# Two 64-row heads in one group of matmuls, by turns, in a two-block transformer kernel

## Chip, core and metric

One Trainium2 chip, one of its cores. The metric is the device time of one execution of the whole kernel, in microseconds (us). All tensors are float32. The kernel runs 256 tokens of width 1024 through two stacked blocks, and reads some 357 MB of weights from memory while it does so.

## What is computed

The first block has two layers. Each has a mixer (retention with 4 heads of 128, and stick-breaking attention with 8 heads of 64) and a gated feed-forward. The second block has two layers of feed-forward, mixer, cross attention to 256 memory rows, and feed-forward. The mixer of its first layer holds forgetting attention (8 heads of 64) and differential attention (4 heads, each of two halves of 64); that of its second layer a short convolution and a banded attention (8 heads of 64). The parts that the change touches, cut to what matters:

```python
# stick-breaking, per 128-query block, 8 heads of d = 64
z = einsum('bqhd,bkhd->bhqk', qb, kk) * d ** -0.5
log_one_minus = where(mask, log_sigmoid(-z), 0)
suffix = cumsum(log_one_minus, reverse) - log_one_minus
A = where(mask, exp(log_sigmoid(z) + suffix), 0)
out = einsum('bhqk,bkhd->bqhd', A, vv)
# differential, 4 heads, j = 0, 1 the two halves of 64
s = einsum('bqhjd,bkhjd->bhjqk', q, k) * 64 ** -0.5
p = softmax(where(allowed, s, -inf))
out = einsum('bhqk,bkhe->bqhe', p[:, :, 0] - lam * p[:, :, 1], v)
```

## The kernel before

**The frame.** Almost all of the work is matmuls of 256 tokens with streamed weights. A weight unit (128 x 1024 numbers) comes by DMA into one of 4 buffers RAW; ScalarE (ACT) rounds it to a high part WH (line 1049), VectorE (DVE) makes the low part WL = RAW - WH (line 1270), and there are 5 pairs WH/WL. TensorE (PE) then multiplies high by high, high by low and low by high, 512 columns each (lines 780 to 782), and adds them up in the PSUM tiles M. A "step" of the plan is three such matmuls for both halves of the tokens, so six instructions.

**The small work.** Attention, transposes and norms are small steps that are laid between those big matmuls. Their results go to four other PSUM banks, AUX. The class `Plan` gives each small step a place in time, `at`, counted in the steps just described, sorts all of them by it, and each engine then works through its own list strictly in that order. ACT and DVE have lists of their own, sorted by `at` plus a delay for the kind of step (`LATER`). Before its matmuls a small step on PE waits until the bank that it got is free (semaphore `aux_out`); when the matmuls are through it raises `aux_full`. The bank is the one whose last user is thought to be done first: each user is taken to hold it until `at` plus `HELD` (3.0 for both kinds of scores below).

**Stick-breaking (`first_mixer`, twice).** A projection leaves two heads on the 128 partitions, the first on rows 0 to 63, the second on rows 64 to 127. For the pair hp (0 to 3) and its head hh (0, 1) there are these steps, with b = e0 + 3.5 * (2 hp + hh):
- `st_z` at b: the scores, three float32 matmuls of 64 rows and 128 columns (lines 874 to 876; each shows as two matmul instructions);
- ACT and DVE turn them into logarithms (lines 1151 to 1157, 1429 to 1434); `st_p` at b + 3.0 splits the result (ACT line 1162, DVE line 1437);
- `st_s` at b + 4.9: the suffix sums on PE (lines 885 to 888), then DVE line 1442, ACT line 1166 and, as `st_a`, DVE line 1446;
- `st_o`, once for the pair, at 11.2 past the first head's b: probabilities by values (lines 900 to 902), the first head into partitions 0 to 63 of the bank, the second into 64 to 127; all three matmuls of the first head come before those of the second. ACT line 1169 and DVE line 1306 empty the bank.

**Differential attention (`even_mixer`, once).** Head h (0 to 3) starts at b = e0 + 5.0 h. Its halves are on rows 0 to 63 and 64 to 127. `df_s` at b and at b + 1.5 are the scores, two float32 matmuls each (line 929 with 128 columns, line 930 with 256). Mask, row maximum (DVE lines 1485 to 1498) and exponential (ACT lines 1200, 1201) follow; `df_p` at b + 4.6 combines both halves (DVE lines 1507 to 1519); `pt` at b + 6.2 turns the result on PE (line 962), `df_o` at b + 7.4 multiplies by the values (lines 973 to 975).

**Forgetting and banded attention (`heads`).** `hg_o` (lines 988, 989) multiplies probabilities by values for two heads as `st_o` does, into the two halves of the partitions of one bank.

Of the kernel before, what the change touches and what calls it, by code (L numbers as in the profile page):

```python
# [14 lines left out]
P = 128  # L15
# [127 lines left out]
class Step:  # L143
    def __init__(self, kind, at, rank):
        self.kind, self.at, self.rank = kind, at, rank
        self.place = self.n = self.bank = self.use = self.hi_n = self.m_n = self.p_n = 0
        self.first_use = False


# [7 lines left out]
class Tmp:  # L157
    def __init__(self, first):
# [6 lines left out]
LATER = {  # L165
    "conv": (0.0, 0.9), "turn": (0.5, 1.0), "tq": (0.5, 0.0), "gains": (0.5, 1.0), "rope": (0.0, 0.6), "ff": (0.0, 0.5),
    "hq": (0.0, 1.3), "ret_s": (0.0, 0.7), "ret_o": (0.9, 1.5), "rg": (0.0, 0.6), "st_z": (0.7, 1.9), "st_p": (0.0, 0.5),
    "st_s": (1.1, 0.6), "st_o": (0.8, 1.2), "df_s": (2.0, 0.8), "hg_s": (2.2, 1.1), "cx_s": (2.2, 1.4), "pt": (0.5, 0.0),
    "cx_pt": (0.6, 0.0), "df_o": (0.8, 0.0), "hg_o": (0.8, 1.2), "cx_o": (1.1, 1.7), "cu1": (0.0, 0.4), "cu_l": (0.0, 0.8),
    "cu2": (0.8, 0.0), "cv": (1.8, 0.0), "su_sin": (0.5, 0.0),  # L170
}
HELD = {"turn": 1.6, "tq": 1.0, "ret_s": 1.2, "ret_o": 1.2, "st_z": 3.0, "st_s": 1.5, "df_s": 3.0, "hg_s": 3.5,
        "cx_s": 2.5}


class Plan:
# [31 lines left out]

    def order(self, ntmp):
        steps = sorted(self.steps, key=lambda s: (s.at, s.rank, s.seq))  # L210
        act, dve = (sorted(steps, key=lambda s: (s.at + LATER.get(s.kind, (0.0, 0.0))[i], s.rank, s.seq)) for i in range(2))
        for i, s in enumerate(steps):
            s.place = i
        counts, use, busy = {}, [0] * 4, [-1e9] * 4
        for i, s in enumerate([s for s in act if s.kind in HALVED]):
            s.hi_n = i + 1
        for i, s in enumerate([s for s in dve if s.kind in ("df_s", "hg_s", "cx_s")]):
            s.m_n = i + 1
        for i, s in enumerate([s for s in dve if s.kind in ("df_p", "hg_p", "cx_p")]):
            s.p_n = i + 1  # L220
        for s in steps:
            counts[s.kind] = s.n = counts.get(s.kind, 0) + 1
            if s.kind in BANKED:
                b = min(range(4), key=lambda b: busy[b])
                use[b] += 1
                s.bank, s.use = b, use[b]
                busy[b] = s.at + HELD.get(s.kind, 1.5)
        ends = [-1] * ntmp
        for b in sorted(self.tmps, key=lambda b: b.first.place):
            b.i = next(i for i in range(ntmp) if ends[i] < b.first.place)  # L230
            ends[b.i] = b.final.place
        for s in steps:
            if s.kind == "mm":
                assert s.src.place < s.place, (s.c.name, s.kt)
        found = [s for s in dve if s.kind in ("ret_v", "hq", "bo_v")]
        assert [s.var for s in act if s.kind == "rsq"] == found
        self.for_pe, self.for_act, self.for_dve = steps, act, dve
# [162 lines left out]
    def first_mixer(self, l, S):  # L400
# [4 lines left out]
        for which, dst in (("rq", QT), ("rk", KT)):  # L405
            c = self.chunk(f"{which}{l}", B, 0, KD, lab)
            s = self.evict_x("rope", c, nm)
# [7 lines left out]
        e0 = c.end + 2.0  # L415
        for h in range(4):
            z = self.add("ret_s", e0 + 2.5 * h)
# [9 lines left out]
        v = self.add("ret_v", e0 + 12.0)  # L427
# [7 lines left out]
        for which, dst, f in (("sq", SQ, 0.125), ("sk", SK, 1.0)):  # L435
            c = self.chunk(f"{which}{l}", B, 0, KD, lab)
            s = self.evict_x("plainx", c, nm)
# [4 lines left out]
        e0 = c.end + 1.0  # L442
        prev = self.spl_prev
        for hp in range(4):
            zs = []
            for hh in range(2):
                i = 2 * hp + hh
                b = e0 + 3.5 * i
                z = self.add("st_z", b)
                z.q, z.k = (x[64 * hh:64 * hh + 64, hp, :] for x in (SQ, SK))  # L450
                z.turned = [self.turned[f"{w}{l}{t}"] for w in ("sq", "sk") for t in range(T)]
                z.sv = sv
                z.x = self.tmp(z)
                z.sp = self.DS[:, i % 2, 0:384]
                g = self.add("st_p", b + 3.0)
                g.z, g.prev = z, prev
                g.sh, g.sl = S["SPL"][:, 0:384], S["SPL"][:, 384:768]
                q = self.add("st_s", b + 4.9)
                q.z, q.p = z, g
                prev = q  # L460
                q.a = self.add("st_a", b + 6.7)
                q.a.s = q
                zs.append(q)
            o = self.add("st_o", b + 7.7)
            o.ss = zs
            for q in zs:
                q.z.x.final = o
            o.v = [SV[:, :, hp * P + hh * 64:hp * P + hh * 64 + 64] for hh in range(2)]
            o.hi, o.lo = A[0][:, 8 + hp, :], A[1][:, 8 + hp, :]
            self.made[f"sb{l}_", hp] = o  # L470
# [4 lines left out]
        for gi, which in enumerate(("gr", "gs")):  # L475
            for n in range(2):
                c = self.chunk(f"{which}{l}", B, 0, KD, lab)
                s = self.evict("gate", c, nm)
# [4 lines left out]
        for n in range(2):  # L483
            c = self.chunk(f"rg{l}", B, 0, KD, lab)
            s = self.evict("rg", c, nm)
# [6 lines left out]
            for j in range(2):  # L492
                k = 4 * n + 2 * j
                blocks = [RET[:, t, (k + q) * P:(k + q + 1) * P] for q in range(2) for t in range(T)]
                self.turn(c.end + 1.5 + 0.5 * j, "rg", s, blocks, A, k, None, f"ra{l}_", k)
        for n in range(2):
# [8 lines left out]
            for j in range(2):  # L505
                s = self.turn(c.end + 2.5 + 0.5 * j, "mer2", m2, None, B, 4 * n + 2 * j, 0.5, f"mg{l}_", 4 * n + 2 * j)
# [31 lines left out]
    def even_mixer(self, S, lab, lab_o):  # L538
# [3 lines left out]
        z = self.add("zero", self.now, 0)  # L542
# [19 lines left out]
        e0 = c.end + 3.5  # L562
        for h in range(4):
            b = e0 + 5.0 * h
            ss = []
            for j in range(2):
                s = self.add("df_s", b + 1.5 * j)
                s.q, s.k = (x[64 * j:64 * j + 64, h, :] for x in (QB, KB))
                s.turned = [self.turned[x] for x in ("bq0", "bq1", "bk0", "bk1")]
                s.vals = bv  # L570
                s.m, s.sm, s.rc = self.small(2), self.small(2), self.small(2)
                s.e = self.tmp(s)
                ss.append(s)
            f = self.add("df_p", b + 4.6)
            f.ss, f.nl = ss, self.small(2)
            t = self.add("pt", b + 6.2)
            ss[1].e.final = t
            t.source, t.maker, t.e = "df_p", f, ss[0].e
            ss[0].e.final = t
            t.x = self.tmp(t)  # L580
            o = self.add("df_o", b + 7.4)
            o.pt = t
            t.x.final = o
            o.v = VB[:, :, h * P:(h + 1) * P]
            o.dst = [BO[:, t_, h * P:(h + 1) * P] for t_ in range(T)]
            o.bs = [BS[:, 4 * t_ + h:4 * t_ + h + 1] for t_ in range(T)]
        v = self.add("bo_v", e0 + 24.5)
# [167 lines left out]
def tensor(e, k):  # L755
    p = k.p
# [3 lines left out]
    for s in p.for_pe:  # L760
        b = s.bank
        if s.kind in BANKED:
            aux = p.AUX[b]
        if s.kind == "mm":
# [12 lines left out]
            out = p.M[c.banks[s.t]][:, 0:s.ncol]  # L777
# [4 lines left out]
            i = e.matmul(out, s.lo, wh, start=False, stop=s.final)  # L782
# [84 lines left out]
        elif s.kind == "st_z":  # L867
# [3 lines left out]
                    e.wait_ge(k.aux_out[x.bank], x.use)  # L871
            if s.use > 1:
                e.wait_ge(k.aux_out[b], s.use - 1)
            e.matmul(aux[:, 0:128], s.k[:, 0:128], s.q[:, 0:128], start=True, stop=True)  # L874
            e.matmul(aux[:, 128:256], s.k[:, 128:256], s.q[:, 128:256], start=True, stop=True)
            e.matmul(aux[:, 256:384], s.k[:, 0:128], s.q[:, 128:256], start=True, stop=True).then_inc(k.aux_full[b], 1)
        elif s.kind == "st_s":
            if s.n == 1:
                e.wait_ge(k.unr_made, 1)
# [9 lines left out]
        elif s.kind == "st_o":  # L889
# [4 lines left out]
            e.wait_ge(k.st_prob, s.ss[1].a.n)  # L894
            if s.use > 1:
                e.wait_ge(k.aux_out[b], s.use - 1)
            for hh in range(2):
                x, v = p.TMP[s.ss[hh].z.x.i], s.v[hh]
                out = aux[64 * hh:64 * hh + 64, :]
                e.matmul(out[:, 0:128], v[:, 0, :], x[:, 0:128], start=True, stop=True)  # L900
                e.matmul(out[:, 128:256], v[:, 0, :], x[:, 256:384], start=True, stop=False)
                i = e.matmul(out[:, 128:256], v[:, 1, :], x[:, 128:256], start=False, stop=True)
            i.then_inc(k.aux_full[b], 1)
        elif s.kind == "cu1":
# [17 lines left out]
        elif s.kind == "df_s":  # L922
# [3 lines left out]
                    e.wait_ge(k.aux_out[x.bank], x.use)  # L926
            if s.use > 1:
                e.wait_ge(k.aux_out[b], s.use - 1)
            e.matmul(aux[:, 0:128], s.q[:, 0:P], s.k[:, 0:128], start=True, stop=True)
            e.matmul(aux[:, 128:384], s.q[:, P:256], s.k[:, 0:256], start=True, stop=True).then_inc(k.aux_full[b], 1)  # L930
        elif s.kind == "hg_s":
            for x in s.turned:
                if x not in seen:
# [42 lines left out]
        elif s.kind == "hg_o":  # L976
# [3 lines left out]
                e.wait_ge(k.m_out[vals.c.banks[1]], vals.c.use[1])  # L980
            if s.use > 1:
                e.wait_ge(k.aux_out[b], s.use - 1)
            for hh in range(2):
                pt, v = s.pts[hh], s.v[hh]
                e.wait_ge(k.aux_out[pt.bank], pt.use)
                x = p.TMP[pt.x.i]
                out = aux[64 * hh:64 * hh + 64, :]
                e.matmul(out[:, 0:256], v[:, 0, :], x[:, 0:256], start=True, stop=False)
                i = e.matmul(out[:, 128:256], v[:, 1, :], x[:, 256:384], start=False, stop=True)
            i.then_inc(k.aux_full[b], 1)  # L990
        elif s.kind == "cx_s":
# [897 lines left out]
```

## Time and profile before

| | |
|---|---|
| time, median of 3 runs | 2081.2 us (2080.53 to 2081.85) |
| the profiled execution's own time | 2080.47 us |
| its span, first to last instruction | 2078.3 us |
| PE matmuls busy | 2056.5 us (99%), 9627 instructions |
| PE weight loads busy | 1683.9 us (81%) |
| DVE busy | 1234.5 us (59%) |
| ACT busy | 1113.1 us (54%) |
| granted TensorE clock | 1.000 |
| DMA, mean | 173 GB/s |

The profile is of one execution. The start times of the matmuls can be relied on; their ends are modelled, and successive matmuls overlap. So a matmul's cost is best read as the distance from its start to the next one's start. A row of the timeline that merges several instructions of one line has their number at its end (x2), and its first number is the start of the first.

### The profile page before, as it was taken

The numbers are of one execution on the slowest core, as the hardware profiler recorded it, in microseconds if no ns is written. First come the engines' busy times: TensorE is split into PE (matmuls) and PEld (weight loads), VectorE is DVE, ScalarE is ACT, GpSimd is POOL, SyncE is SP. The second block draws the span as 40 slices with busy tenths as digits, with TensorE's granted clock in tenths as the row PEclk, the third lists the DMA queues.
The fourth block names the chain that finished last, engine by engine and source line by source line (L and its number), as shares of the span: only waits on it lengthen the run. The fifth ranks groups of instructions, "written<-read, shape, count | busy, mean of one in ns | idle before, by whom it ended". The sixth has DMA issues, their size and how long they took to land.

```text
span 2078.3 us, 25155 instructions
## 1 busy us (share of the span) xinstructions
PE 2056.5 (99%) x9627; PEld 1683.9 (81%) x9627; DVE 1234.5 (59%) x1721; ACT 1113.1 (54%) x1682; POOL 36.3 (2%) x60
## 2 busy tenths in 40 slices
PE   8999999999999999999999999999999999999999
PEld 6877888888778888888887888888888888788887
DVE  6576665565657555655557765655555466655553
ACT  5565544445665544654456665544444465665442
POOL 0000100000000000000000000000000000000000
PEclk9999999999999999999999999999999999999999
DMA  7545566555545665566564344665666563545553
GB/s 249 156 139 167 177 186 185 186 170 170 148 157 179 203 189 191 183 189 187 187 164 141 123 156 145 185 183 188 185 185 187 188 192 127 176 136 163 184 188 131
DMA packets 258215, 359.76 MB, mean 173 GB/s; under 512 B 16909, under 2 KB 152289, under 8 KB 258097
## 3 DMA queue, kind: packets, MB, share of 16 engines
q1 hardware_dynamic: 256016, 352.75, 54.5%
q0 software_dynamic: 2080, 5.41, 0.8%
q8 instruction: 77, 1.26, 0.2%
q14 instruction: 42, 0.34, 0.0%
HBM read 357.04 MB, written 1.06 MB: 172 GB/s over the span
## 4 chain that ended last, share of the span: by engine, by line
PE 95%; DVE 2%; ACT 1%; issue 1%; POOL 0%; DMA 0%; SPq 0%; DVEq 0%; ACTq 0%
PE M L780 29%; PE M L782 28%; PE M L781 28%; PE AUX L822 3%; PE AUX L836 1%; DVE WL L1270 1%; PE AUX L1022 1%; PE AUX L1000 1%; PE AUX L947 1%; ACT WH L1049 1%; PE AUX L962 0%; PE AUX L874 0%; DMA RAW<-in_w_in 0%; PE AUX L953 0%; DVE RET L1453 0%
## 5 line engine op out<-in xcount | busy, mean ns | idle before, releaser
L1270 DVE TENSOR_TENSOR WL<-RAW,WH 128x1024 fp32r<-128x1024 f32 x669 | 815.9, 1222 | 660.7 <-ACT WH L1049 657.9
L1049 ACT ACTIVATE WH<-RAW 128x1024 fp32r<-128x1024 f32 x669 | 706.3, 1058 | 670.5 <-PE M L782 664.1
L780 PE MATMUL M<-WH,Bh 128*128 128x512 f32 x1792 | 719.9, 402 | 3.9 <-DVE WL L1270 3.9
L782 PE MATMUL M<-WH,Bl 128*128 128x512 f32 x1792 | 700.4, 391 | 0.0
L781 PE MATMUL M<-WL,Bh 128*128 128x512 f32 x1792 | 699.5, 390 | 0.0
L780 PEld LDWEIGHTS M<-WH,Bh 128*128 128x128 f32 x1792 | 337.2, 188 | 73.5 <-DVE WL L1270 4.9
L782 PEld LDWEIGHTS M<-WH,Bl 128*128 128x128 f32 x1792 | 336.7, 188 | 72.6
L781 PEld LDWEIGHTS M<-WL,Bh 128*128 128x128 f32 x1792 | 337.7, 188 | 63.4
L1078 ACT ACTIVATE AS<-M,KEEP 128x256 f32<-128x256 f32 x132 | 55.3, 470 | 101.0 <-PE M L782 97.6
L780 PE MATMUL M<-WH,MTh 128*128 128x512 f32 x128 | 55.1, 430 | 0.0
L782 PE MATMUL M<-WH,MTl 128*128 128x512 f32 x128 | 50.5, 395 | 0.0
L781 PE MATMUL M<-WL,MTh 128*128 128x512 f32 x128 | 50.5, 394 | 0.0
L1328 DVE SCALAR_TENSOR_TENSOR X<-M,X 128x512 f32<-128x512 f32 x48 | 30.9, 686 | 20.8 <-PE M L782 20.7
L1099 ACT ACTIVATE Bh<-AUX,GTt 128x256 fp32r<-128x256 f32 x48 | 22.8, 474 | 29.0 <-PE AUX L822 29.0
L1295 DVE SCALAR_TENSOR_TENSOR Bl<-AUX,GTt,Bh 128x256 fp32r<-128x256 f32 x48 | 23.2, 483 | 25.3 <-ACT Bh L1100 25.3
L822 PEld LDWEIGHTS AUX<-CC,X 128*128 128x128 f32 x192 | 22.9, 144 | 15.2 <-issue 9.2
L780 PE MATMUL M<-WH,FA0h 128*128 128x512 f32 x88 | 34.5, 392 | 0.0
L780 PE MATMUL M<-WH,GA0h 128*128 128x512 f32 x88 | 34.5, 392 | 0.0
L780 PE MATMUL M<-WH,LA0h 128*128 128x512 f32 x88 | 34.5, 392 | 0.0
L780 PE MATMUL M<-WH,GA1h 128*128 128x512 f32 x88 | 34.5, 392 | 0.0
L780 PE MATMUL M<-WH,LA1h 128*128 128x512 f32 x88 | 34.3, 390 | 0.0
L780 PE MATMUL M<-WH,FA1h 128*128 128x512 f32 x88 | 34.3, 390 | 0.0
(405 smaller groups left out, 2515.4 us busy)
## 6 DMA issues: line engine op xcount, KB each, us to landing
RAW<-in_ffn_w_in SPq DMA_DIRECT2D x352, 256.0 KB, 3.2
RAW<-in_w_in SPq DMA_DIRECT2D x104, 512.0 KB, 3.8
RAW<-in_w_gate_up SPq DMA_DIRECT2D x176, 256.0 KB, 3.3
RAW<-in_ffn_w_out SPq DMA_DIRECT2D x88, 512.0 KB, 3.6
RAW<-in_w_down SPq DMA_DIRECT2D x44, 512.0 KB, 3.7
RAW<-in_x_w_kv SPq DMA_DIRECT2D x32, 512.0 KB, 3.6
RAW<-in_even_w_in SPq DMA_DIRECT2D x24, 512.0 KB, 3.9
RAW<-in_odd_w_in SPq DMA_DIRECT2D x24, 512.0 KB, 3.9
```

Source lines behind the costliest of these rows:

```text
L780: e.matmul(out, s.hi, wh, start=s.at0, stop=False)
L781: e.matmul(out, s.hi, wl, start=False, stop=False)
L782: i = e.matmul(out, s.lo, wh, start=False, stop=s.final)
L822: tr = e.transpose(aux[:, i * P:(i + 1) * P], x, ident)
L836: tr = e.transpose(aux[:, j * P:(j + 1) * P], x[:, j * P:(j + 1) * P], ident)
L947: e.matmul(out, s.q[:, q0:q0 + P], s.k[:, 0:kw], start=True, stop=False)
L1049: e.activation(p.WH[:, h, 0:s.size], p.RAW[:, i, 0:s.size], ACT.Copy).then_inc(k.w_hi, 1)
L1078: e.activation(s.silu[t], banks[t][:, 0:256], ACT.Silu, scale=r[t]).then_inc(k.silu_made, 1)
L1099: e.activation(s.hi[0], aux[:, 0:256], ACT.Copy, scale=s.gain[0])
L1270: e.tensor_tensor(p.WL[:, h, 0:s.size], p.RAW[:, s.u % NRAW, 0:s.size], hi.bitcast(F32), ALU.subtract).then_inc(k.w_lo, 1)
L1295: e.scalar_tensor_tensor(out=s.lo[0], in0=aux[:, 0:256], scalar=s.gain[0], in1=s.hi[0].bitcast(F32), op0=ALU.mult, op1=ALU.subtract)
L1328: e.scalar_tensor_tensor(out=x, in0=banks[t][:, :], scalar=s.scale, in1=x, op0=ALU.mult, op1=ALU.add).then_inc(k.m_out[c.banks[t]], 1)
```

## The change

The two heads (or halves) of a pair are scored in one group. Both steps now have the first one's `at`; what the second had more (3.5 or 1.5) is kept in a new number `late`, which is added for the order on ACT and DVE and for how long the bank is taken to be held, but not for the order on PE. The first step only waits on PE; the second, which knows the first as its `mate`, waits too and then issues the matmuls of both by turns, into the two banks. In `st_o` and `hg_o` the matmuls of the two heads also go by turns, and the two waits of `hg_o` stand before the first matmul. The arithmetic is the same.

```diff
@@ order
-        act, dve = (sorted(steps, key=lambda s: (s.at + LATER.get(s.kind, (0.0, 0.0))[i], s.rank, s.seq)) for i in range(2))
+        act, dve = (sorted(steps, key=lambda s: (s.at + s.late + LATER.get(s.kind, (0.0, 0.0))[i], s.rank, s.seq)) for i in range(2))
-                busy[b] = s.at + HELD.get(s.kind, 1.5)
+                busy[b] = s.at + s.late + HELD.get(s.kind, 1.5)
@@ first_mixer
-                z = self.add("st_z", b)
+                z = self.add("st_z", e0 + 7.0 * hp)
+                z.late = 3.5 * hh
+                z.mate = zs[0].z if hh else None
@@ even_mixer
-                s = self.add("df_s", b + 1.5 * j)
+                s = self.add("df_s", b)
+                s.late = 1.5 * j
+                s.mate = ss[0] if j else None
@@ tensor, st_z
-            e.matmul(aux[:, 0:128], s.k[:, 0:128], s.q[:, 0:128], start=True, stop=True)
-            e.matmul(aux[:, 128:256], s.k[:, 128:256], s.q[:, 128:256], start=True, stop=True)
-            e.matmul(aux[:, 256:384], s.k[:, 0:128], s.q[:, 128:256], start=True, stop=True).then_inc(k.aux_full[b], 1)
+            if s.mate is not None:
+                z, x = s.mate, p.AUX[s.mate.bank]
+                e.matmul(x[:, 0:128], z.k[:, 0:128], z.q[:, 0:128], start=True, stop=True)
+                e.matmul(aux[:, 0:128], s.k[:, 0:128], s.q[:, 0:128], start=True, stop=True)
+                e.matmul(x[:, 128:256], z.k[:, 128:256], z.q[:, 128:256], start=True, stop=True)
+                e.matmul(aux[:, 128:256], s.k[:, 128:256], s.q[:, 128:256], start=True, stop=True)
+                e.matmul(x[:, 256:384], z.k[:, 0:128], z.q[:, 128:256], start=True, stop=True).then_inc(k.aux_full[z.bank], 1)
+                e.matmul(aux[:, 256:384], s.k[:, 0:128], s.q[:, 128:256], start=True, stop=True).then_inc(k.aux_full[b], 1)
@@ tensor, st_o
-            for hh in range(2):
-                x, v = p.TMP[s.ss[hh].z.x.i], s.v[hh]
-                out = aux[64 * hh:64 * hh + 64, :]
+            xs = [p.TMP[q.z.x.i] for q in s.ss]
+            outs = [aux[64 * hh:64 * hh + 64, :] for hh in range(2)]
+            for x, v, out in zip(xs, s.v, outs):
                 e.matmul(out[:, 0:128], v[:, 0, :], x[:, 0:128], start=True, stop=True)
+            for x, v, out in zip(xs, s.v, outs):
                 e.matmul(out[:, 128:256], v[:, 0, :], x[:, 256:384], start=True, stop=False)
+            for x, v, out in zip(xs, s.v, outs):
                 i = e.matmul(out[:, 128:256], v[:, 1, :], x[:, 128:256], start=False, stop=True)
@@ tensor, df_s
+                e.matmul(x[:, 0:128], z.q[:, 0:P], z.k[:, 0:128], start=True, stop=True)
+                e.matmul(aux[:, 0:128], s.q[:, 0:P], s.k[:, 0:128], start=True, stop=True)
+                e.matmul(x[:, 128:384], z.q[:, P:256], z.k[:, 0:256], start=True, stop=True).then_inc(k.aux_full[z.bank], 1)
+                e.matmul(aux[:, 128:384], s.q[:, P:256], s.k[:, 0:256], start=True, stop=True).then_inc(k.aux_full[b], 1)
@@ tensor, hg_o
-            for hh in range(2):
-                pt, v = s.pts[hh], s.v[hh]
+            for pt in s.pts:
                 e.wait_ge(k.aux_out[pt.bank], pt.use)
...
+            for x, v, out in zip(xs, s.v, outs):
                 e.matmul(out[:, 0:256], v[:, 0, :], x[:, 0:256], start=True, stop=False)
+            for x, v, out in zip(xs, s.v, outs):
                 i = e.matmul(out[:, 128:256], v[:, 1, :], x[:, 256:384], start=False, stop=True)
```

## Rows read from the trace of the kernel before

**Rows 1.** The page, part 4: engines' shares of the chain that ended last.
```profile
PE 95%; DVE 2%; ACT 1%; issue 1%; POOL 0%; DMA 0%; SPq 0%; DVEq 0%; ACTq 0%
```
**Rows 2.** Timeline of PE round one `st_z`: start us, us, instruction, count.
```profile
102.19 0.39 PE L781 MATMUL M<-WL,Bh 128*128 128x512 f32 x1
...
103.10 0.39 PE L782 MATMUL M<-WH,Bl 128*128 128x512 f32 x1
103.42 0.49 PE L874 MATMUL AUX<-SQ,SK 64*128 64x128 f32 x2
...
103.97 0.38 PE L876 MATMUL AUX<-SQ,SK 64*128 64x128 f32 x2
104.28 0.50 PE L780 MATMUL M<-WH,Bh 128*128 128x512 f32 x1
...
105.08 0.39 PE L780 MATMUL M<-WH,Bh 128*128 128x512 f32 x1
```
**Rows 3.** Timeline of PE round one `df_s`.
```profile
1112.08 0.39 PE L782 MATMUL M<-WH,Bl 128*128 128x512 f32 x1
...
1114.05 0.40 PE L780 MATMUL M<-WH,Bh 128*128 128x512 f32 x1
```
**Rows 4.** Source line 874: weight loads, duration in ns, lowest, median, highest.
```profile
L874 PEld LDWEIGHTS AUX<-SQ,SK x32: 182/184/186, 103.4 to 573.1; 64*128 64x128 f32 x32
```
**Rows 5.** Timeline of PE in one `st_o`.
```profile
124.64 0.43 PE L900 MATMUL AUX<-TMP,SV 128*64 128x128 f32 x2
...
124.91 0.32 PE L900 MATMUL AUX<-TMP,SV 128*64 128x128 f32 x1
...
125.12 0.27 PE L902 MATMUL AUX<-TMP,SV 128*64 128x128 f32 x1
...
125.40 0.38 PE L902 MATMUL AUX<-TMP,SV 128*64 128x128 f32 x2
```
**Rows 6.** Timeline of PE in one `hg_o`.
```profile
1202.34 0.66 PE L988 MATMUL AUX<-TMP,VA 128*64 128x256 f32 x4
...
1203.14 0.50 PE L780 MATMUL M<-WH,XA0h 128*128 128x512 f32 x1
```
**Rows 7.** Timelines of DVE and PE: a bank emptied by `st_o`, the next `st_z`.
```profile
126.96 0.42 DVE L1306 TENSOR_TENSOR MA0l<-AUX,MA0h 128x256 fp32r<-128x256 f32 x1 [0.54 <-ACT MA0h L1169]
...
129.93 0.48 PE L874 MATMUL AUX<-SQ,SK 64*128 64x128 f32 x2
```
**Rows 8.** Timelines of ACT, DVE and PE at the end of stick-breaking; brackets: idle time, releaser.
```profile
152.50 1.06 ACT L1049 ACTIVATE WH<-RAW 128x1024 fp32r<-128x1024 f32 x1 [0.84 <-PE M L782]
...
152.01 0.42 DVE L1446 TENSOR_TENSOR TMP<-TMP,CC 128x256 f32<-128x256 f32 x1
...
150.59 0.48 PE L874 MATMUL AUX<-SQ,SK 64*128 64x128 f32 x2
...
153.04 0.43 PE L900 MATMUL AUX<-TMP,SV 128*64 128x128 f32 x2
...
160.92 0.44 PE L885 MATMUL AUX<-SPL,UNR 128*128 128x384 f32 x1 [0.49 <-DVE SPL L1437]
```
**Rows 9.** Timelines of DVE, ACT and PE in differential attention.
```profile
1115.40 1.23 DVE L1270 TENSOR_TENSOR WL<-RAW,WH 128x1024 fp32r<-128x1024 f32 x1 [2.31 <-ACT WH L1049]
...
1125.32 0.48 DVE L1519 SCALAR_TENSOR_TENSOR TMP<-TMP,SM 128x256 f32<-128x256 f32 x1
...
1128.62 0.68 ACT L1110 ACTIVATE QA<-AUX,GTt 64x512 f32<-64x512 f32 x1 [0.42 <-PE AUX L836]
...
1125.87 0.54 PE L962 MATMUL AUX<-CC,TMP 128*128 128x128 f32 x3
...
1137.90 0.55 PE L962 MATMUL AUX<-CC,TMP 128*128 128x128 f32 x3 [1.38 <-DVE TMP L1519]
```

More of the change, by code:

```diff
@@ L146, in __init__ @@
         self.place = self.n = self.bank = self.use = self.hi_n = self.m_n = self.p_n = 0
+        self.late, self.mate = 0.0, None
         self.first_use = False
@@ L928, in tensor @@
                 e.wait_ge(k.aux_out[b], s.use - 1)
-            e.matmul(aux[:, 0:128], s.q[:, 0:P], s.k[:, 0:128], start=True, stop=True)
-            e.matmul(aux[:, 128:384], s.q[:, P:256], s.k[:, 0:256], start=True, stop=True).then_inc(k.aux_full[b], 1)
+            if s.mate is not None:
+                z, x = s.mate, p.AUX[s.mate.bank]
+                e.matmul(x[:, 0:128], z.q[:, 0:P], z.k[:, 0:128], start=True, stop=True)
+                e.matmul(aux[:, 0:128], s.q[:, 0:P], s.k[:, 0:128], start=True, stop=True)
+                e.matmul(x[:, 128:384], z.q[:, P:256], z.k[:, 0:256], start=True, stop=True).then_inc(k.aux_full[z.bank], 1)
+                e.matmul(aux[:, 128:384], s.q[:, P:256], s.k[:, 0:256], start=True, stop=True).then_inc(k.aux_full[b], 1)
         elif s.kind == "hg_s":
@@ L982, in tensor @@
                 e.wait_ge(k.aux_out[b], s.use - 1)
-            for hh in range(2):
-                pt, v = s.pts[hh], s.v[hh]
+            for pt in s.pts:
                 e.wait_ge(k.aux_out[pt.bank], pt.use)
-                x = p.TMP[pt.x.i]
-                out = aux[64 * hh:64 * hh + 64, :]
+            xs = [p.TMP[pt.x.i] for pt in s.pts]
+            outs = [aux[64 * hh:64 * hh + 64, :] for hh in range(2)]
+            for x, v, out in zip(xs, s.v, outs):
                 e.matmul(out[:, 0:256], v[:, 0, :], x[:, 0:256], start=True, stop=False)
+            for x, v, out in zip(xs, s.v, outs):
                 i = e.matmul(out[:, 128:256], v[:, 1, :], x[:, 256:384], start=False, stop=True)
```

## The prediction

> **What bounds the kernel now.** I read the chain of waits by engine first, since it says whose time the end is made of: 95% of it is TensorE [rows 1], at a granted clock of 1.000 throughout. So what PE's queue loses or gains is the kernel's time, unless PE then has to wait for VectorE or ScalarE. Next I read PE's timeline by distances between starts, because a modelled end says nothing. The big matmuls run at (103.10 - 102.19) / 4 = 0.2275 us each [rows 2]. With that pitch the price of a small step can be read as what it adds: from the last big matmul before `st_z` (103.10) to the fourth after it (105.08) are 1.98 us, of which 4 x 0.2275 = 0.91 belong to the big ones, so `st_z` costs 1.07 us; followed two matmuls further, until the pitch is regular again, it is 1.08. It has only six instructions, 0.11 us apart inside the group (the fifth starts at 103.97, 0.55 after the first: one longer first step of 0.21 and three of 0.11) [rows 2]. The rest is the way in (0.32 instead of 0.23) and out (104.28 to 105.08: 0.80 for three big ones instead of 0.68). For `df_s` the same reckoning gives 114.05 - 112.08 = 1.97, less 0.91, 1.06 us, 1.07 when followed further [rows 3].
>
> **The change part by part.**
>
> *Scores of stick-breaking.* 4 pairs in 2 layers, 8 pairs; each has two groups now, 2.16 us. Afterwards there is one. What it costs depends on whether matmuls on rows 0 to 63 and on rows 64 to 127 run beside each other, into two banks. No row shows that. Bounds: entirely beside each other, one group of 1.08 plus an offset; one after the other with a free change, 1.08 + 6 x 0.11 = 1.74. What lies nearest are two heads in two halves of the *output* partitions. In `hg_o` eight passes, four of them with 256 columns, need 1203.14 - 1202.34 = 0.80 us [rows 6], where one after the other, at twice 0.11 for twice the columns, they would need 4 x 0.22 + 4 x 0.11 = 1.32. Those halves do run beside each other, some 0.014 us apart. I take the same for the rows: 1.08 + 0.01 a pair, a gain of 1.07, 8 x 1.07 = 8.5 us on PE.
>
> *Scores of differential attention.* 4 pairs, 2 x 1.07 before. Beside each other the gain is 1.06 each, 4.2 us on PE; one after the other 1.07 + 2 x 0.11 + 2 x 0.22 = 1.73, a gain of 0.41.
>
> *`st_o` by turns.* Here the two heads already overlap, but late: the second head's first matmul starts at 124.91, when the first head's third has started, and after that both advance together, the last pass starting at 125.40 + 0.11 = 125.51, 0.87 us after the first [rows 5]. In `hg_o`, where the first head has four passes and not six, both are through in the 0.80 us above, so the second must start at once. So an instruction seems to be let in when the one four places before it has started. By turns, the second head's first pass is the third in the queue and starts at once; the group is then one head's own length, 0.16 + 4 x 0.11 + 0.01 = 0.61, a gain of 0.26, 8 x 0.26 = 2.1 us. Bounds: 0 to 0.26 each, below zero only in the last rival.
>
> The Trainium skill speaks against this step. The row shows line 900 of the second head at 124.91, before line 902 of the first at 125.12, though the program has all of the first head's before it [rows 5]. The page TensorE: Matmul & The Clock Gate (What overlaps and what doesn't) says that matmuls start and end strictly in program order, and that weight loads go ahead during a matmul only when the row group differs, which it does not for two halves of the output. By the page the eight `st_o` would gain nothing and may lose (the last rival); by the rows the order is kept only within each half, and the sum has 2.1 us. I go by the rows. The same skill, TensorEngine Tiling (Key Properties), says that a change of tiling mode drains the engine, and the 0.32 on the way in agrees; that cost is what one group in place of two saves.
>
> *`hg_o` by turns and its waits.* The two heads already overlap from the start [rows 6]: 0. Moving the second head's wait ahead of the first head's matmuls could cost at most the 0.2 us for which the first one would have run alone, and in the eight groups the second head's bank is emptied just before; I take 0.
>
> *Banks.* The second head of a pair now waits for its bank 3.5 steps (3.5 x 6 x 0.2275 = 4.8 us) earlier, or 1.5 steps (2.0 us), with all later PE work behind it in the queue. Going through the rule by which banks are given, with the longer holding time, the tightest case is the third pair of stick-breaking: its second head gets the bank that `st_o` of the first pair has used 2.8 steps before. DVE empties that one at 126.96 + 0.42 = 127.38; the pair's group stands at 129.93 [rows 7]. 2.5 us remain: 0. In differential attention the same rule gives no tighter case.
>
> *What is late next.* The data of the first head must be ready 1.07 us sooner as PE sees it, because the second head's group no longer stands between. Most deadlines have room, but not all.
> - Last pairs of stick-breaking, in each layer. `st_o` of the third pair starts at 153.04, DVE line 1446 for it ends at 152.01 + 0.42 = 152.43: room 0.61. The group at 150.59 between goes away [rows 8], so PE waits some 0.5 us. Then the suffix sums at 160.92 already wait 0.49 us. The chain to them starts with the ACT conversion at 152.50, which had been idle for 0.84 us waiting for PE [rows 8]; it can come forward by 0.84 and no more, while PE has come forward by 1.07 + 0.26 = 1.33. The two are not added, the later one takes up the earlier: 0.49 us lost, 2 x 0.49 = 1.0 us.
> - Differential attention. DVE has no gap between 1115.40 and the end of line 1519 at 1125.80, and PE transposes its result at 1125.87 [rows 9]: no room. DVE's run starts from a big matmul before 1112, so it comes forward by the first pair's 1.06 only; the second pair's gain becomes a wait. The third transpose waits 1.38 us already (1137.90). What leads to it is ACT, busy from 1128.62 after an idle 0.42 for PE [rows 9]: it comes forward by that 0.42 more and the rest of the third pair's gain is lost. The fourth pair's 1.06 comes after that wait; before the fourth transpose there are some 0.2 us of room and DVE busy before it, so of its gain I count only 0.17. Together 1.06 + 0.42 + 0.17 = 1.65 of the 4.2 us. Bounds: 1.0 (the first pair alone) and 4.2.
>
> *The sum.* 8.5 + 2.1 - 1.0 + 1.65 = 11.3 us. The profiled execution took 2080.47 us, 2.2 outside its span, and goes to 2069.2; the median shown is 0.7 higher, so I forecast 2081.2 - 11.3 = 2069.9 us. ACT, DVE and DMA keep their work and, but for those waits, follow PE.
>
> **The rivals.**
> - *No new waits:* what ACT and DVE do comes forward with PE, because the second head's scores lie ready sooner and fill their idle time. 8.5 + 4.2 + 2.1 = 14.8: 2066.4. For it: both idle more than a third of the time. Against: their order is fixed and they are unbroken exactly before the deadlines [rows 9].
> - *Rows don't overlap:* the two heads' passes run one after the other in one group. 8 x (2.16 - 1.74) + 4 x 0.41 = 5.0 on PE; the waits then take only about 0.5 of it, since 0.42 + 0.26 is under the 0.84 of the suffix chain. With 2.1 from `st_o`: 6.7, so 2074.5. For it: no row shows row halves side by side. Against: output halves do.
> - *Paced by ACT and DVE:* PE's gain in both attention stretches turns into waits like the 0.49 and 1.38 us ones. Only what follows the last wait remains, under 2 us: about 2080, no change that can be told. For it: two waits stand there already. Against: of the eight suffix sums of a layer PE waits for the last alone, and for one of the first three transposes.
> - *Slower: a change of tile between successive matmuls exposes a weight load.* The load of line 874 takes 0.184 us [rows 4], hidden now. By turns there are 5 changes in a pair of `st_z` and 3 in one of `df_s`, and 4 and 2 more than now in `st_o` and `hg_o`: 8 x 5 + 4 x 3 + 8 x 4 + 8 x 2 = 100. Rows then don't overlap (5.0 saved), and 100 x 0.184 = 18.4 are paid: +13.4, 2094.6 us. It decides from 5.0 / 100 = 0.05 us a change on. For it: the first `st_z` step, 0.21 instead of 0.11, looks like such a load. Against: passes of both heads alternate in rows 5 without it. By the skill's sentence on row groups, cited above, the output halves would pay it and the rows would not.
>
> **How the numbers follow.** Forecast 0.62 (its own range 2067.5 to 2072), no new waits 0.10, rows don't overlap 0.14, paced 0.07, slower 0.07. The range holds the first three, 0.86: from 2066.4 less 0.6 for what the order of waits may add, 2065.8, to 2074.5 plus 1.5 for losses in between, 2076.0. Faster by over 0.2% (4.2 us, about what a measurement of this kernel tells from no change) 0.86; within it 0.07; slower 0.07.
>
> **What would show it.** PE's timeline at the first pair: lines of both heads within 0.02 us of each other, and one way in and out where there were two, the group costing about 1.09; if the passes stand 0.11 apart, rows don't overlap. `st_o` 0.61 long from first to last start. A wait before line 900 of the third pair of some 0.5 us, none before the group at 129.93, about 1 us of wait before the second transpose and 2 before the third in differential attention. The forecast is wrong if a pair costs more than 1.74, or if PE waits for `aux_out` before a pair.

## The result: faster, by the time that was forecast

| | before | changed |
|---|---|---|
| median | 2080.86 us (2080.52 to 2081.85, 4 runs) | 2069.23 us (2067.88 to 2070.11, 4 runs) |
| profiled span | 2078.3 us | 2065.7 us |
| PE matmuls busy | 2056.5 us | 2042.6 us |
| matmul instructions | 9627 | 9627 |

The ratio is 0.9946, 95% interval 0.9934 to 0.9958: 11.6 us less, where 11.3 were forecast. The changed kernel's four runs themselves spread over 2.2 us, so the medians alone could not tell 11.6 from 11.3; the traces below can.

The end is still made of PE, with a little more of the others. The page of the changed kernel, part 4, answers to [rows 1]:

```profile
PE 94%; DVE 3%; ACT 2%; issue 1%; POOL 0%; DMA 0%; SPq 0%; DVEq 0%; ACTq 0%
```

A pair of `st_z`, from PE's timeline of the changed kernel (start us, us, instruction, count), answers to [rows 2]. Lines 881, 883 and 885 are the first head's matmuls, 882, 884 and 886 the second's; the big matmuls are now lines 785 to 787.

```profile
101.60 0.39 PE L787 MATMUL M<-WH,Bl 128*128 128x512 f32 x1
101.92 0.37 PE L881 MATMUL AUX<-SQ,SK 64*128 64x128 f32 x1
101.92 0.37 PE L882 MATMUL AUX<-SQ,SK 64*128 64x128 f32 x1
102.13 0.27 PE L881 MATMUL AUX<-SQ,SK 64*128 64x128 f32 x1
102.14 0.27 PE L882 MATMUL AUX<-SQ,SK 64*128 64x128 f32 x1
102.24 0.27 PE L883 MATMUL AUX<-SQ,SK 64*128 64x128 f32 x1
102.25 0.27 PE L884 MATMUL AUX<-SQ,SK 64*128 64x128 f32 x1
...
102.58 0.27 PE L885 MATMUL AUX<-SQ,SK 64*128 64x128 f32 x1
102.58 0.27 PE L886 MATMUL AUX<-SQ,SK 64*128 64x128 f32 x1
102.79 0.50 PE L785 MATMUL M<-WH,Bh 128*128 128x512 f32 x1
```

Read the starts in twos: the heads are less than 0.01 us apart at each step. From the last big matmul to the next one are 1.19 us for twelve instructions, where six took 1.18 before. The second head costs nothing.

`st_o` of the first pair, same timeline, answers to [rows 5]. The rows are merged by line, and each of the first three holds four instructions, two of each head:

```profile
120.97 0.44 PE L910 MATMUL AUX<-TMP,SV 128*64 128x128 f32 x4
121.24 0.39 PE L912 MATMUL AUX<-TMP,SV 128*64 128x128 f32 x4
121.46 0.39 PE L914 MATMUL AUX<-TMP,SV 128*64 128x128 f32 x4
121.78 0.50 PE L785 MATMUL M<-WH,Bh 128*128 128x512 f32 x1
```

From the first start to the next big matmul are 0.81 us. Before they were 1.07: 0.87 to the last pass and a way out of 0.20.

The price is in waits. PE's waits over the whole span (engine, line, waited for, us in total, times, longest):

```profile
PE AUX L978 <- DVE TMP L1536: 3.0, 3, 1.6
...
PE AUX L910 <- DVE TMP L1463: 1.0, 2, 0.5
...
PE AUX L895 <- DVE SPL L1454: 0.7, 2, 0.4
PE AUX L978 <- DVE TMP L1547: 0.5, 1, 0.5
PE AUX L1039 <- DVE YA0l L1326: 0.5, 1, 0.5
```

The first row (the transposes of differential attention) was 1.38 us once. The second (`st_o`) was nothing. The third (the last suffix sums) was 0.49 twice. The fourth, 0.5 us, was there before with the same length. The last, a product of the cross attention, is new.

**Where the time came from.** The big matmuls are the same 8016 in both kernels, in the same order, except where they make room for small steps. The difference between the start of the n-th of them in one trace and in the other is a curve, and its steps are what each place gave or took:

| stretch (us of before) | PE forward by | forecast |
|---|---|---|
| 0 to 20 (nothing changed there) | 1.48 | - |
| 20 to 1000, stick-breaking, twice | 9.83 | 9.6 |
| 1099 to 1200, differential and forgetting attention | 2.04 | 1.65 |
| 1200 to the end | -0.73 | 0 |

The first 20 us aren't the change. PE waits there for the first inputs and units, and over the traces of the eleven experiments below the same number ran from 1.05 forward to 0.78 back. Without it the profiled change is 11.14 us. In what follows "net" is that number for each kernel: PE's shift against the trace of before from 20 us to the end.

### The profile page after: what moved, and what is told of

It reads as the page before. It is cut to its first block, busy times and chain, and to the rows that moved or that the text cites. A ratio compares the mean times of both kernels' runs of the same rounds, so it can differ in the third digit from the quotient of the medians.

```text
span 2065.7 us, 25169 instructions
## 1 busy us (share of the span) xinstructions
PE 2042.6 (99%) x9627; PEld 1674.2 (81%) x9627; DVE 1234.0 (60%) x1721; ACT 1111.7 (54%) x1682; POOL 36.3 (2%) x60
## 3 DMA queue, kind: packets, MB, share of 16 engines
HBM read 357.04 MB, written 1.06 MB: 173 GB/s over the span
## 4 chain that ended last, share of the span: by engine, by line
PE 94%; DVE 3%; ACT 2%; issue 1%; POOL 0%; DMA 0%; SPq 0%; DVEq 0%; ACTq 0%
PE M L785 28%; PE M L787 28%; PE M L786 28%; PE AUX L827 3%; DVE WL L1287 1%; PE AUX L841 1%; PE AUX L1039 1%; PE AUX L1017 1%; ACT WH L1066 1%; PE AUX L963 1%; PE AUX L978 0%; PE AUX L969 0%; DVE RET L1470 0%; DVE SM L1436 0%; PE AUX L1004 0%
```

## The experiments

My theory: two heads on different halves of the rows, or writing to different halves of the partitions, run beside each other; an instruction is let in when the one four before it has started, and ACT's and DVE's deadlines take part of the gain. The rivals are that the gain is the saved way in and out of a group and not the overlap, that turns expose weight loads, and that the attention stretches are paced by ACT and DVE. Each run has the kernel before beside it on the same chip, with medians of 2079.9 us (E1 to E4), 2080.45 (E5 to E8) and 2080.17 (E9 to E11). The ratios go by these.

**E1, turns alone.** The kernel before with the diff's `st_o` and `hg_o` only (`hg_o` likewise):

```diff
-for hh in range(2):
-    x, v = p.TMP[s.ss[hh].z.x.i], s.v[hh]
+for x, v, out in zip(xs, s.v, outs):
...
+for x, v, out in zip(xs, s.v, outs):
```

> The kernel before, with only st_o and hg_o by turns. Overlap theory (two halves of the output partitions advance beside each other, and an instruction is let in when the one four places before it has started): st_o 0.61 us from first to last start instead of 0.87, 8 x 0.26 = 2.1 us on PE, of which the third pair's 0.26 in each layer goes into the suffix sums' wait: 1.6 us, 2079.3. hg_o unchanged. Strict order theory (a change of half exposes a load): st_o 1.0 us or longer, slower than before by 2 us or more.

Median 2079.2 us against 2079.9 (0.9996, 0.9987 to 1.0006): not to be told from nothing. The trace tells it: net 1.58 us, in steps of 0.25 to 0.30 at each `st_o`, and in each layer some 0.26 given back at the last suffix sums. `hg_o` did not move. These are the theory's numbers (1.6 us, forecast from 0.26 a group). Strict order, by which `st_o` would have got longer, is out.

**E2, `st_z` alone.** The changed kernel with `df_s`, `st_o` and `hg_o` as before.

```diff
-s = self.add("df_s", b)
-s.late = 1.5 * j
-s.mate = ss[0] if j else None
+s = self.add("df_s", b + 1.5 * j)
```

> Only st_z grouped and by turns; df_s, st_o and hg_o as before. Overlap theory: 8 x 1.07 = 8.5 us on PE, less 0.24 in each layer at the last suffix sums (PE 1.07 forward, the chain to it 0.84): 8.1 us, about 2072.8. If rows do not overlap and only the way in and out is saved: 8 x 0.42 = 3.4 us, about 2077.5.

2072.98 us (0.9966, 0.9953 to 0.9979). Over the stretch of stick-breaking PE comes forward by 8.15 us, where 8.1 were expected. The forecast of the total, 2072.8, holds only by luck. The kernel before was 1 us faster on this chip, so the medians are 6.9 us apart and not 8.1, and the trace loses 1.63 us elsewhere, in differential attention that is as before. Its timeline of PE and the granted clock (stretch, length, busy of PE, PEld, DVE, ACT, POOL, then PEclk) show why:

```profile
1129.01 0.55 PE L970 MATMUL AUX<-CC,TMP 128*128 128x128 f32 x3 [1.38 <-DVE TMP L1527]
...
1132.84 0.63 PE L981 MATMUL AUX<-VB,TMP 128*128 128x128 f32 x2
```

```profile
1129.00:1130.00 1.00, 0.99 (x6) 0.82 (x7) 1.00 (x1) 0.41 (x1) 0.00 (x0) 1.00 0.04 14
1130.00:1131.00 1.00, 1.00 (x4) 0.59 (x4) 0.96 (x4) 0.09 (x1) 0.00 (x0) 0.81 0.00 0
1131.00:1132.00 1.00, 1.00 (x4) 0.71 (x4) 0.90 (x5) 0.88 (x4) 0.00 (x0) 0.50 0.59 199
...
1133.00:1134.00 1.00, 1.00 (x8) 1.00 (x6) 0.97 (x4) 0.00 (x0) 0.00 (x0) 0.50 0.08 29
1134.00:1135.00 1.00, 1.00 (x6) 0.83 (x6) 1.00 (x1) 0.72 (x5) 0.00 (x0) 0.98 0.00 0
```

After the wait of 1.38 us that stands in the kernel before too, the granted clock fell to 0.50 (1.2 GHz of 2.4) for 3.4 us, and two passes of line 981 took 0.63 where they took 0.38. In the trace of before the same wait left the clock at 1.00. It doesn't look like an accident of the one trace: the mean granted clock was 0.999 in four of E2's five executions, and only the fastest (2072.40 us) had 1.000, where the executions of before beside them all had 1.000.

**E3, one group, but one head after the other.**

```diff
 z, x = s.mate, p.AUX[s.mate.bank]
-# z's first, s's first, z's second, s's second, z's third, s's third
+# z's three, then s's three (df_s: z's two, then s's two)
```

> The changed kernel, but the matmuls of a pair of st_z (6 instructions a head) and of df_s (4 a head) issued one head after the other, still in one group. If an instruction is let in when the one four places before has started: st_z's second head starts with the first head's third pass, about 0.32 us late, the group 1.4 instead of 1.09, df_s's starts at once. 8 x 0.31 = 2.5 us more than the changed kernel, less some 0.3 at the deadlines: 2071.4. If the turns do not matter: as the changed kernel, 2069.2. If only turns make them overlap: 12 x 0.66 = 7.9 more, 2077.

2071.33 us (0.9958, 0.9943 to 0.9972), net 8.55 us, 2.6 less than the changed kernel. PE's timeline of E3, a pair of `st_z` (lines 881 to 883 first head, 884 to 886 second) and the start of a pair of `df_s` (943 and 944, 945 and 946):

```profile
102.82 0.48 PE L881 MATMUL AUX<-SQ,SK 64*128 64x128 f32 x2
103.14 0.27 PE L882 MATMUL AUX<-SQ,SK 64*128 64x128 f32 x1
103.15 0.37 PE L884 MATMUL AUX<-SQ,SK 64*128 64x128 f32 x1
103.25 0.27 PE L882 MATMUL AUX<-SQ,SK 64*128 64x128 f32 x1
103.36 0.27 PE L884 MATMUL AUX<-SQ,SK 64*128 64x128 f32 x1
103.37 0.27 PE L883 MATMUL AUX<-SQ,SK 64*128 64x128 f32 x1
```

```profile
1095.60 0.37 PE L943 MATMUL AUX<-KB,QB 64*128 64x128 f32 x1
1095.61 0.37 PE L945 MATMUL AUX<-KB,QB 64*128 64x128 f32 x1
```

The seventh instruction (the first of line 884) starts 0.006 us after the third; with four to a head, as in `df_s`, the fifth starts 0.013 us after the first. A pair of `st_z` costs 0.32 us more than by turns, 8 x 0.32 = 2.6, and `df_s` the same within 0.01. So the turns made a difference with six instructions a head and none with four; other lengths were not run. Line 884 starts before the second of line 882 and both of line 883, which stand ahead of it in the program. The order of the starts is kept within a half of the array only, which is not what the Trainium skill says (TensorE: Matmul & The Clock Gate, What overlaps and what doesn't: matmuls start and end in program order).

**E4, both heads on the same rows.** The second head of each pair of scores reads rows 0 to 63, so it scores the first head's numbers again.

```diff
-z.q, z.k = (x[64 * hh:64 * hh + 64, hp, :] for x in (SQ, SK))
+z.q, z.k = (x[0:64, hp, :] for x in (SQ, SK))
-s.q, s.k = (x[64 * j:64 * j + 64, h, :] for x in (QB, KB))
+s.q, s.k = (x[0:64, h, :] for x in (QB, KB))
```

> The changed kernel, but the second head of each st_z and df_s pair reads the first head's rows 0 to 63 (so it scores the first head's numbers again). Overlap theory: on the same rows nothing runs beside, a pair costs 1.09 + 6 x 0.11 = 1.75, 12 x 0.66 = 7.9 us more on PE than the changed kernel, of which up to 2.6 were waits before and cost nothing: 5.3 to 7.9 more, 2074.5 to 2077. If the gain is only the saved way in and out: no difference, 2069.2.

2075.23 us (0.9977, 0.9968 to 0.9987), net 4.61, 6.5 less than the changed kernel. PE's timeline, the same place:

```profile
103.80 0.48 PE L881 MATMUL AUX<-SQ,SK 64*128 64x128 f32 x2
104.13 0.38 PE L882 MATMUL AUX<-SQ,SK 64*128 64x128 f32 x2
104.35 0.38 PE L883 MATMUL AUX<-SQ,SK 64*128 64x128 f32 x2
...
105.33 0.50 PE L785 MATMUL M<-WH,Bh 128*128 128x512 f32 x1
```

After a first step of 0.21 the twelve starts are 0.11 us apart. The pair costs 0.66 us more than with two halves of the rows, which is 6 x 0.11. The overlap belongs to the halves of the rows. The saved way in and out alone is worth what it was reckoned at, 0.42 a pair. E4 says nothing about the rival of exposed loads, since it has no change of rows. The changed kernel's pair puts that one out: there the rows change from each matmul to the next, and it is the shortest of all.

**E5, the bank of the second `cx_o`.** `cx_o` is the product of the cross attention at line 1039. Its wait is far from anything that was changed, so I went through the banks. Two were thought to be free at exactly the same time (in steps of the plan: a transpose at 796.4 + 1.0, the first `cx_o` at 795.9 + 1.5), and the lower number wins. The changed groups had exchanged the numbers of the banks, and the second `cx_o` now got the first one's, which empties later.

```diff
+# first cx_o of the first layer
+o.held = 1.6
-busy[b] = s.at + s.late + HELD.get(s.kind, 1.5)
+busy[b] = s.at + s.late + (s.held or HELD.get(s.kind, 1.5))
```

> The changed kernel; the first cx_o of the first cross attention is taken to hold its bank for 1.6 steps instead of 1.5, so that the next one gets again the bank that it had before the change. If the 0.7 us that PE loses at the second cx_o (0.45 us wait on line 1326 of DVE) comes from the bank alone: the loss is gone, all else stays to 0.05 us, 2068.5. If it comes from something that arrives later there: no difference.

2068.26 us (0.994, 0.9926 to 0.9953); net 11.77, and after 1200 us nothing is lost where 0.73 was. The medians of the two can't be told apart; the traces can. PE's timeline of the changed kernel, and of E5 (its line 1040):

```profile
1241.22 1.96 PE L1039 MATMUL AUX<-TMP,VX 128*128 128x256 f32 x8 [0.45 <-DVE YA0l L1326]
```

```profile
1241.76 1.89 PE L1040 MATMUL AUX<-TMP,VX 128*128 128x256 f32 x8
```

**E6, differential attention's transposes later.** `pt` and `df_o` of every head 1.2 steps later.

```diff
-t = self.add("pt", b + 6.2)
+t = self.add("pt", b + 7.4)
-o = self.add("df_o", b + 7.4)
+o = self.add("df_o", b + 8.6)
```

> The changed kernel with pt and df_o of differential attention 1.2 steps (1.6 us) later. Deadline theory: PE's waits before the transposes (0.7, 1.55 and 0.7 us, 3.0 in sum) go, PE does big matmuls instead; the bank of the second cx_o also returns to what it was: 3.0 + 0.7 = 3.7 less than the changed kernel, 2065.5. If ACT and DVE pace this stretch as a whole the waits move to the transposes' new place: 0.7 less, 2068.5.

2069.93 us (0.9949, 0.9937 to 0.9962), slower than both forecasts. The net is 11.16, in the stretch of differential attention 1.23 us forward instead of 2.04; that the total is as for the changed kernel comes from the second `cx_o`, whose 0.73 us were not lost here. The waits before the transposes went, and worse ones came behind them, 1.43 us before the first head's `df_o` and 2.70 before the second's. PE's and ACT's timelines of E6:

```profile
1116.69 0.49 PE L978 MATMUL AUX<-CC,TMP 128*128 128x128 f32 x3
1121.94 0.49 PE L989 MATMUL AUX<-VB,TMP 128*128 128x128 f32 x2 [2.70 <-ACT TMP L1231]
```

```profile
1117.98 0.69 ACT L1099 ACTIVATE TMP<-M,KEEP 128x512 f32<-128x512 f32 x1
...
1120.48 1.04 ACT L1066 ACTIVATE WH<-RAW 128x1024 fp32r<-128x1024 f32 x1
1121.42 0.47 ACT L1231 ACTIVATE TMP<-AUX 128x384 f32<-128x384 f32 x1
```

The transposed scores lie ready at 1117.2. ACT copies them at 1121.42, because with the later `at` the copy had slipped behind a projection's eviction (four operations, from 1117.98) and a conversion. My expectation moved PE's step and forgot that ACT's moves with it.

**E7 and E11, `st_o` and the last suffix sums later** (0.7 and 0.5 steps), otherwise the changed kernel. E11 is E7 once more, on the chip of E9 and E10.

```diff
-q = self.add("st_s", b + 4.9)
+q = self.add("st_s", b + (4.9 if (hp, hh) != (3, 1) else 5.4))
-q.a = self.add("st_a", b + 6.7)
+q.a = self.add("st_a", b + (6.7 if (hp, hh) != (3, 1) else 7.2))
-o = self.add("st_o", b + 7.7)
+o = self.add("st_o", b + 8.4)
```

> The changed kernel with st_o 0.7 steps (1.0 us) later and the last suffix sums of each layer 0.5 steps (0.7 us) later. Deadline theory: waits of 0.1 + 0.5 before st_o and 0.35 before the last suffix sums go in each layer, 1.8 us in both, and the second cx_o has its old bank (0.7): 2.5 less, 2066.7. Paced by ACT and DVE: 0.7 less, 2068.5.

> E7 once more, beside E9 and E10 on the same chip: 2066.3; its spread says what a difference between them is worth.

2066.34 us (0.9933, 0.9921 to 0.9946) and on another chip 2066.4 (the same ratio); net 13.89 and 13.85. Stick-breaking gives 11.78 instead of 9.83 us, 1.95 more where 1.8 were expected, and the second `cx_o` had its bank back by the way. The deadlines were real, and PE could pass them by doing big matmuls first. One wait of 0.7 us at a pair came in, for a bank, at the fourth pair of the first layer (PE's timeline of E7):

```profile
140.74 0.34 PE L881 MATMUL AUX<-SQ,SK 64*128 64x128 f32 x1 [0.70 <-DVE MA0l L1323]
```

The pair takes the bank of an `st_o` that now stands 2.1 steps ahead and not 2.8. That alone is 0.96 us, and the changed kernel had 1.96 us of room there; the rest is that VectorE empties the bank 4.9 us after that `st_o` has started, where it was 3.1.

**E8, all three together:** the diffs of E5, E6 and E7.

> The edits of the last three together. Deadline theory: 3.0 + 1.8 + 0.7 = 5.5 less than the changed kernel, 2063.7, and the granted clock never falls, since no wait over 0.6 us is left after the start. Paced theory: 2068.5.

2068.71 us (0.9943, 0.9931 to 0.9956), net 11.52. The number is that of the paced theory (2068.5), but the trace doesn't bear it out: stick-breaking gave the full 11.78 us as in E7. What is missing is E6's loss and the clock, once more at half for 3.4 us after the 2.7 us wait, which cost 1.5 us beside E6. The mean granted clock was 0.999 in all five executions.

```profile
1122.00:1124.00 2.00, 2.00 (x8) 1.17 (x8) 1.90 (x9) 1.59 (x5) 0.00 (x0) 0.50 0.71 250
```

**E9 and E10, differential attention again, on E7.** The second to fourth heads' `pt` and `df_o` 0.6, 1.2 and 0.6 steps later, in E10 on ACT too. In E9 `late` takes the same amount off again, so that the order on ACT and DVE is kept, and the time for which the bank is taken to be held too:

```diff
+late_h = (0.0, 0.6, 1.2, 0.6)[h]
-t = self.add("pt", b + 6.2)
+t = self.add("pt", b + 6.2 + late_h)
+t.late = -late_h    # E9 only; the same for df_o at b + 7.4
```

> E7 (st_o and the last suffix sums later) and, in differential attention, pt and df_o of the second, third and fourth head 0.6, 1.2 and 0.6 steps (0.8, 1.6, 0.8 us) later on PE, while ACT's order stays as it was. In e6 the copy of pt had slipped behind the eviction of the next projection on ACT, and PE then waited 2.7 us for it at df_o. If that slip was the whole cause, the waits of 0.7, 1.55 and 0.7 us go: 3.0 less than E7, 2063.4. If ACT and DVE pace the stretch whatever the order: as E7.

> As E9, but the same steps are later on ACT too; the second head's copy (734 less 0.2) now just stays ahead of the eviction of the projection. If the slip behind the eviction is what cost: 2063.4 as E9. If any later copy costs: between E7 and E9, some 2065.

E9: 2065.03 us (0.9926, 0.9913 to 0.994), net 15.25, the lowest median of all. E10: 2066.38 (0.9934, 0.9922 to 0.9947), net 14.17, like E11 beside it. The intervals of the three overlap; it is their traces, one each, that differ. In E9 the waits before the transposes fell from 3.0 to 0.9 us, but PE came forward by 1.4 more than in E11 and not by 3.0. The 0.9 that stayed and a new wait of 0.4 before the first scores of forgetting attention are 1.3 of the missing 1.6. E10 has no wait before these transposes, but 1.29 and 0.66 before `df_o` and the same 0.4.

The 1.29 is not the order on ACT. PE's and ACT's timelines of E10:

```profile
1116.63 0.46 PE L990 MATMUL AUX<-VB,TMP 128*128 128x128 f32 x2 [1.29 <-ACT QA L1129]
```

```profile
1114.74 0.49 ACT L1232 ACTIVATE TMP<-AUX 128x384 f32<-128x384 f32 x1
...
1115.80 0.68 ACT L1129 ACTIVATE QA<-AUX,GTt 64x512 f32<-64x512 f32 x1
```

The copy of the transposed scores is through at 1115.23, and PE starts 1.4 us later, when line 1129 is through at 1116.48. That line empties the bank of a projection's transpose, which by the rule for the banks is the one that this `df_o` gets in E10. In E9, where `late` also shortens the time of holding, it gets another bank and doesn't wait. Without the 1.29 E10's waits in this stretch would be 1.1 us and E9's are 1.2, so the pair doesn't show that keeping ACT's order is worth anything by itself. Only the 0.66 is a copy that came late. That a copy behind an eviction costs stands on E6.

## Why the prediction was right

- *Scores of stick-breaking.* 1.07 a pair was forecast, carried over from the halves of the output partitions, which were seen side by side, to halves of the rows, which were not. It was an assumption, and it held. A pair costs 1.087 us, forecast 1.09; the offset of a head is 0.007 and not 0.014. E2 gave 8.15 for 8.1, and E4 showed that it is the rows.
- *`st_o`.* 0.25 to 0.30 a group for 0.26. The rule of four, which it was worked out from, held in E3 too, in a place where it had not been read.
- *`hg_o`.* 0, as said.
- *Waits at the end of stick-breaking.* 0.5 us before line 910 of the third pair in each layer, as said. At the suffix sums 0.95 of the 1.34 us (1.07 + 0.27) were kept, 0.84 was forecast. Forecast for the stretch 9.6, measured 9.83; the 0.11 in each layer is most of the difference.
- *Differential attention, the term that was mis-sized.* The second transpose came forward by 1.12 (forecast 1.06), the third by 1.98 (1.48), the fourth by 2.17 (1.65). The step that was too small is the third's, "it comes forward by that 0.42 more". ACT's idle time of 0.42 before 1128.62 was not its only slack: before, ACT also came to the second head's copy 0.90 us after the transpose had started, being busy, and now 0.58 us after it (1113.44 and 1114.02). That is 0.32 more. From that copy on ACT works without a pause, as before, but for the same gap, and this was 0.53 us by the distance of starts (1128.00 to 1128.62, now 1115.25 to 1115.34) and not 0.42. Together they are 0.85 of the 0.86 us by which the third transpose gained on the second. So PE's waits came out shorter than forecast: 0.72 us before the second transpose for about 1, and 1.55 before the third for about 2. The changed kernel's PE timeline, and the copy on ACT before and in the changed kernel:

```profile
1113.44 0.55 PE L978 MATMUL AUX<-CC,TMP 128*128 128x128 f32 x3 [0.72 <-DVE TMP L1536]
...
1124.61 0.55 PE L978 MATMUL AUX<-CC,TMP 128*128 128x128 f32 x3 [1.55 <-DVE TMP L1536]
...
1134.35 0.55 PE L978 MATMUL AUX<-CC,TMP 128*128 128x128 f32 x3 [0.68 <-DVE TMP L1536]
```

```profile
1126.77 0.49 ACT L1214 ACTIVATE TMP<-AUX 128x384 f32<-128x384 f32 x1
```

```profile
1114.02 0.49 ACT L1231 ACTIVATE TMP<-AUX 128x384 f32<-128x384 f32 x1 [0.58 <-PE AUX L978]
```

- *Banks.* No new wait at a pair, as said. The tightest was the fourth pair and not the third: in the changed kernel 1.96 us of room against 2.25, and it was the fourth that waited in E7. And I followed the banks of the steps that move and not those after them; the 0.73 us at the second `cx_o` were missed. That loss nearly cancels with the 0.4 us too few in differential attention and the 0.2 too few in stick-breaking (9.83 + 2.04 - 0.73 = 11.14). So the sum is better than its terms, which is luck.
- *The rivals.* That the rows don't overlap is refuted by E4, and exposed loads by the pair in the timeline. Pacing as a whole is refuted by E7 for stick-breaking. In differential attention it stays open how far it holds: 3.0 us of waits are there, and E9 got 1.4 of them.

## To carry to other kernels

Two float32 matmul chains that used different halves of the rows, or of the output partitions, cost as much as one when they stood in one group with four instructions of the first ahead of the second; with six they had to be dealt out by turns. The gain of a shorter PE queue is what its next deadlines allow: list for each step when its data is ready and when PE comes, take off what is removed in between, and move the late ones. When a step moves on PE, look at what it then stands behind on the engine that evicts it: in E6 a copy that slipped behind an eviction cost 2.7 us. And look at every buffer that is given out by a rule after the changed place, ties above all.

## What the hardware showed that was not expected

- A wait of 1.38 us on an otherwise full PE was followed by half the clock for 3.4 us in the trace of E2, but not in others with the same wait (before) or with one of 1.55 (changed) or 2.7 us (E6). After 2.7 us it was there in E8. It cost 1.6 us in E2. The mean granted clock on record for each execution says how often: 0.999 in four of E2's five, all of E8's and four of E1's ten, 0.999 and 0.998 in two of E6's five, 0.999 in one of the nine of before beside E5 to E8, and 1.000 in all others that are listed. Only the traces show where it fell. E1's four at 0.999 have a median of 2079.84 us, its six at 1.000 one of 2078.71. What decides it isn't known. It isn't the whole spread either: the changed kernel's four runs differ by 2.2 us, all at 1.000.
- Going over to a group of 64 rows has a price of its own, 0.38 us. A `df_o` before has six float32 instructions with 128 columns too, but on all 128 rows:

```profile
1140.48 0.39 PE L782 MATMUL M<-WH,Bl 128*128 128x512 f32 x1
1140.71 0.38 PE L973 MATMUL AUX<-VB,TMP 128*128 128x128 f32 x2
...
1141.30 0.47 PE L780 MATMUL M<-WH,Bh 128*128 128x512 f32 x1
...
1142.08 0.40 PE L780 MATMUL M<-WH,Bh 128*128 128x512 f32 x1
```

  It costs 1142.08 - 1140.48 - 0.91 = 0.69 us (0.68 to 0.69 in all four), an `st_z` 1.07. The way in is 0.23 us there and 0.318 for the 64 rows, the first step inside 0.11 and 0.21, and the last start stands 0.03 ahead of the next big matmul and not 0.20. One group in place of two is worth 0.42 us before any overlap, and this is nearly all of it.
